# Filter spectra of the 256-step stream from even and odd lags, and expert weights in groups of four rows

## The chip, the cores and the metric

The kernel runs on one core of a Trainium2 chip. The metric is the device time of one execution in microseconds (us); the time of a kernel is the median of its runs. TensorE (PE in the profile, its weight loads are PEld), VectorE (DVE), ScalarE (ACT), GpSimd (POOL) and SyncE (SP) run their own instruction streams and meet at semaphores. The DMA engines move data between HBM and SBUF.

## What is computed

A two-layer step over two streams, a context of 128 tokens and a latent grid of 256 tokens, both 1024 wide, all in float32. Layer 0 mixes tokens with long convolutions (Hyena), layer 1 with a gated scan (RG-LRU); after each comes a mixture of 16 experts, of which a token takes two. The parts of the reference that matter here:

```python
def hyena_filter_spectrum(length, f_w1, f_b1, f_freq, f_w2, f_b2, f_w3):
    ...
    h = (h @ f_w3.astype(f32)).reshape(length, 2, HY_ORDER, D_MODEL)
    deltas = jnp.abs(jnp.linspace(MIN_DECAY, MAX_DECAY, D_MODEL, dtype=f32))
    h = h * jnp.exp(-t[:, :, None, None] * deltas)
    h_fwd = h[:, 0]
    h_bwd = h[1:, 1]
    norm = jnp.sum(jnp.abs(h_fwd), axis=0) + jnp.sum(jnp.abs(h_bwd), axis=0) + FILTER_EPS
    k = jnp.concatenate([h_fwd, jnp.zeros((1, HY_ORDER, D_MODEL), f32), h_bwd[::-1]], axis=0) / norm
    return jnp.fft.rfft(k, axis=0)

def moe_ffn(h, router_w, router_bias, w1, w3, w2):
    ...
    def expert_block(args):
        xblk, e = args
        return (jax.nn.silu(xblk @ w1[e]) * (xblk @ w3[e])) @ w2[e]
```

The kernel computes the transforms as matrix products with cosine and sine matrices (constants named `lag`, `fwd`, `inv`).

## The kernel before

**Tiles.** Tokens lie in three tiles of 128: tile 0 is the context, tiles 1 and 2 the latent stream. `halves` is the large SBUF buffer that holds weights, filters and spectra; `PS` is PSUM, eight banks of 512 floats per partition. A float32 `mm` is two matmul instructions in the trace, so 10 calls read as x20.

**Layer 0, the filters.** The filters are made in four units (convolution 0 or 1, channels 0-511 or 512-1023). For unit i, `filter_rows` (PE, six products, one per tile and direction) is windowed by DVE into `fa` and `fb` (sums and differences of the two directions). ACT takes absolute values (`filter_abs`, L559 and L560), DVE their larger (`filter_larger`, L1344), PE adds them up (`filter_sums`, 12 small products), DVE inverts (`filter_norm`). `spectrum(i)` on PE multiplies `fa` and `fb` by the lag matrices: for each of three frequency tiles ft and r = 0 (real, from `fa`), 1 (imaginary, from `fb`) one result ("K", i, ft, r) of 128x512. For ft = 0 (context) it is one product, for ft = 1 and 2 (latent) two products that accumulate, over lags 0-127 and 128-255. ACT copies all six results to `spec[i]` (`emptied`, L477).

**What sets the order.** Each engine runs a hand-written list (`mixer0` has one for PE, one for ACT, one for DVE). The results of the filter and transform work share banks 3 to 7: `pool_plan` numbers the uses in PE's order, use u gets bank 3 + u % 5, and PE's `take` for use u waits until use u - 5 has been emptied by the engine that the plan names. So the sixth result of a spectrum waits for the copy of its first, and the sums after it for the copy of its second. Between the units PE runs `in_tile(ct)` (24 input projection tiles), `ada` (modulation rows) and, from ct = 5, `z_rows`, `transform` and `inverse`; DVE multiplies the spectra in `multiply`. Unit 0's spectrum stands before `norm_spread(0)`, unit 1's after `mod_columns(0)`, unit 2's and 3's after `in_tile(1)` and `in_tile(3)`. On ACT the copies of unit 1 stand behind `modulate(0)` (L514) and those of units 2 and 3 behind `in_tile` and `filter_abs`.

**The experts.** SP loads per expert six pieces of 2 MB: the two halves of w1 and w3 alternating, then w2, each as [128 partitions x 4096 floats], into eight ring slots, each as soon as the slot's last reader is done. The view `(k p j) n -> p k (j n)` with j = 2 gives every partition two pairs of neighbouring rows, that is two stretches of 8 KB. PE for expert e multiplies by w1 and w3 (64 matmul instructions, L752 `halves,hT`), gathers the next expert's tokens out of `h` (12, `h,hT`), transposes hid (4) and gate picks (3), multiplies by w2 (32), transposes the gathered tokens `xg` (4, L756) and combines (16, `hT,misc`). `xg` columns must come in the order in which the weights' rows lie, so `chunk` picks every second column of a 256-column stretch. An expert with over 64 tokens has an extra pass. ACT writes `h` from transposed tokens in `token_tile` (L717), six per layer, the first of them ahead of the router's exponential.

```python
order = (("moe_w1", 0), ("moe_w3", 0), ("moe_w1", 1), ("moe_w3", 1), ("moe_w2", 0), ("moe_w2", 1))
MOE_RELEASE = ("w13_last", "w13_last", "w13_last", "w13_last", "w2_first", "w2_mm")
```

Of the kernel before, what the change touches and what calls it, by code (L numbers as in the profile page):

```python
# [11 lines left out]
ALU = mybir.AluOpType  # L12
ACT = mybir.ActivationFunctionType
AX = mybir.AxisListType.X

P = 128
# [48 lines left out]

def constants():
# [16 lines left out]
    for name, n in (("lat", LAT), ("ctx", CTX)):  # L83

        k = np.arange(n) if n == CTX else np.concatenate([np.arange(0, n, 2), np.arange(1, n, 2)])
# [8 lines left out]
        at = np.pi * (2 * k[None, :] + 1) * np.arange(n)[:, None] / (2 * n)  # L94
        lag.insert(0, np.stack([np.cos(at), -sign * np.sin(at)], 1).reshape(n // P, P, 2 * n).transpose(1, 0, 2)
                   .reshape(P, 2 * n * n // P))
# [4 lines left out]
    for n in (CTX, LAT):  # L101
        t = np.linspace(0.0, 1.0, n, dtype=np.float32)[:, None]
        w = np.float32(2.0 * math.pi / n) * np.arange(n, dtype=np.float32)[:, None]
        a = (bands * w).astype(np.float32)
        feats.append(np.concatenate([t, np.cos(a), -np.sin(a)], -1))
        window.append(np.exp(-t * deltas))
# [89 lines left out]
def pool_plan():  # L196
# [4 lines left out]
    spectrum = lambda i: [("act", ("K", i, ft, r)) for ft in range(NT) for r in range(2)]  # L201
# [21 lines left out]
def program(nc, A, y_prompt, y_sample, new_state):  # L223
    where, (pool, pool_order, pool_count) = plan(), pool_plan()
    with ExitStack() as ctx:
# [66 lines left out]
        lags = halves[:, W_AT + 6656:W_AT + 7936]  # L292
# [62 lines left out]
        def _(sp):  # L355
# [50 lines left out]
            for l in range(LAYERS):  # L406
# [10 lines left out]
                w = {m: A[m].rearrange("l e (k p j) n -> p (l e) k (j n)", p=P, j=2) for m in ("moe_w1", "moe_w3", "moe_w2")}  # L417
                order = (("moe_w1", 0), ("moe_w3", 0), ("moe_w1", 1), ("moe_w3", 1), ("moe_w2", 0), ("moe_w2", 1))

                def expert(c, e):  # L420
                    name, half = order[c]
                    return w[name][:, l * NE:(l + 1) * NE][:, bass.ds(e, 1), 2 * half:2 * half + 2, :]

                def load_expert(c, r, e, *released):
                    slot = moe_slot(r, c)
                    load(("moe", l, slot), expert(c, e), ring[:, slot, :].rearrange("p (o k n) -> p o k n", o=1, k=2),
# [34 lines left out]
        def _(act):  # L461
# [88 lines left out]
            def spectrum(i):  # L550
                for ft in range(NT):
# [151 lines left out]
            for l in range(LAYERS):  # L703
# [11 lines left out]
                def token_tile(i):  # L715
                    act.wait_ge(S("tok_mm"), before("tok_mm", l) + i + 1)
                    a.activation(h[:, i // 2, i % 2 * HALF:i % 2 * HALF + HALF], PS[:, 2 + i, :], ACT.Copy) \  # L717
                        .then_inc(S("tok"), 1)
# [31 lines left out]
        def _(pe):  # L750
# [53 lines left out]
            def spectrum(i):  # L804
                lat = lags[:, 2 * CTX:].rearrange("p (k r f) -> p k r f", k=2, r=2)
                pe.wait_ge(S("pl_dve"), pool["rows", i, NT - 1, 1][2])
                for ft in range(NT):
                    for r, src in enumerate((fa, fb)):
                        bank = take(("K", i, ft, r))
                        if ft == 0:  # L810
                            last = mm(PS[:, bank, :], lags[:, CTX * r:CTX * r + CTX], src[:, 0, :], True, True)
                        else:
                            for k in range(2):
# [1032 lines left out]
```

## Time and profile before

| | |
|---|---|
| median of 3 runs | 1675.11 us (1672.68 to 1677.9) |
| the profiled execution | 1676.27 us |
| its span in the trace | 1674.5 us |
| PE busy / DVE busy / ACT busy | 1555.0 / 713.3 / 331.6 us |
| moved by DMA | 495.66 MB in 83949 packets |

The span is the time from the first to the last instruction; 1.8 us lie outside. Layer 0's mixer ends at about 351 us, its experts fill 380 to 948 us, layer 1's mixer 950 to 1135 us, its experts 1165 to 1656 us. A row of the timeline is a start, a length, engine, line, operation and tiles, merged over neighbours of one kind; in brackets stands the idle time ahead and what ended it.

### The profile page before, as it was taken

How to read it: one execution, taken by the hardware profiler on the slowest of the kernel's cores; microseconds unless marked ns; L12 is line 12 of the kernel's file. 1: busy time of each engine (PE TensorE's matmuls, PEld its weight loads, DVE VectorE, ACT ScalarE, POOL GpSimd, SP SyncE). 2: the span in 40 equal slices, each digit the busy share in tenths (PEclk: the TensorE clock that was granted, in tenths of full speed). 3: DMA queues.
4: the chain of work that ended last, by engine and by line, in shares of the span. 5: the costliest groups of instructions: out<-in, count | busy, mean ns of one | idle time of the engine just before them, and what ended most of it. 6: DMA issues, size and time to landing. Idle time of an engine off the chain costs nothing.

```text
span 1674.5 us, 21517 instructions
## 1 busy us (share of the span) xinstructions
PE 1555.0 (93%) x7910; PEld 699.9 (42%) x7911; DVE 713.3 (43%) x2050; ACT 331.6 (20%) x539; POOL 0.2 (0%) x4
## 2 busy tenths in 40 slices
PE   6999999978999999999989799896999998999996
PEld 3454555543343333333333355453333333333333
DVE  3325665352424434334343548725334342434343
ACT  4322222030101111010101357413011110111111
POOL 0000000000000000000000000000000000000000
PEclk9999999989999999999999899997999999999998
DMA  9438776830858999999968501424799995999993
GB/s 351 153 106 299 264 262 226 349 153 1 354 249 336 423 422 422 422 422 422 422 267 350 201 0 51 201 101 163 288 413 422 422 422 240 423 422 421 423 423 132
DMA packets 83949, 495.66 MB, mean 296 GB/s; under 512 B 4465, under 2 KB 21121, under 8 KB 28225
## 3 DMA queue, kind: packets, MB, share of 16 engines
q1 hardware_dynamic: 82432, 489.33, 72.3%
q10 hardware_dynamic: 1472, 5.72, 1.0%
q8 instruction: 31, 0.51, 0.1%
q14 instruction: 14, 0.11, 0.0%
HBM read 493.45 MB, written 1.58 MB: 296 GB/s over the span
## 4 chain that ended last, share of the span: by engine, by line
PE 83%; DVE 6%; DMA 5%; ACT 3%; issue 2%; SPq 0%; DVEq 0%; ACTq 0%
PE PS L752 81%; DMA halves<-in_moe_w 4%; PE PS L756 2%; DMA halves<-in_ada_w 1%; DVE misc L1760 1%; ACT hT L543 1%; DVE xc L1702 1%; DVE misc L1522 0%; DVE halves L1522 0%; DVE halves L1513 0%; DVE halves L1515 0%; DVE halves L1514 0%; DVE hT L1750 0%; ACT hT L528 0%; ACT hT L514 0%
## 5 line engine op out<-in xcount | busy, mean ns | idle before, releaser
L752 PE MATMUL PS<-halves,hT 128*64 128x512 f32 x3072 | 677.0, 596 | 22.4 <-ACT hT L543 17.2
L752 PEld LDWEIGHTS PS<-halves,hT 128*64 128x64 f32 x3072 | 225.4, 137 | 442.5 <-issue 432.8
L752 PE MATMUL PS<-hT,halves 128*128 128x384 f32 x640 | 218.7, 497 | 8.4 <-ACT halves L626 6.5
L1702 DVE SCALAR_TENSOR_TENSOR xc<-PS,MOD,xc 128x128 f32<-128x128 f32 x592 | 195.8, 409 | 37.4 <-PE PS L752 37.4
L752 PEld LDWEIGHTS PS<-hT,halves 128*128 128x128 f32 x640 | 121.5, 193 | 106.7 <-issue 23.0
L1750 DVE TENSOR_TENSOR hT<-hT,PS 128x512 f32<-128x512 f32 x32 | 22.0, 688 | 279.3 <-ACT hT L528 279.3
L752 PE MATMUL PS<-halves 128*128 128x384 f32 (+1 forms) x336 | 118.5, 512 | 0.7 <-ACT pre L573 0.7
L752 PE MATMUL PS<-h,hT 128*64 128x512 f32 x408 | 108.8, 667 | 7.4 <-issue 3.9
L1760 DVE COPY misc<-PS 128x512 f32<-128x512 f32 x32 | 22.1, 692 | 216.6 <-PE PS L752 216.6
L528 ACT ACTIVATE hT<-PS 128x512 f32<-128x512 f32 x32 | 19.1, 597 | 449.6 <-PE PS L752 449.6
L752 PE MATMUL PS<-hT,misc 64*128 64x384 f32 x512 | 91.2, 495 | 3.6
L752 PEld LDWEIGHTS PS<-halves 128*128 128x128 f32 x336 | 63.4, 190 | 53.9 <-issue 17.1
L756 PEld LDWEIGHTS PS<-cst,hT 128*128 128x128 f32 x408 | 50.9, 185 | 58.9 <-issue 55.1
L548 ACT ACTIVATE hT<-PS 128x512 f32<-128x512 f32 x32 | 19.1, 597 | 244.8 <-PE PS L756 244.8
L756 PE MATMUL PS<-cst,hT 128*128 128x128 f32 x408 | 65.6, 296 | 1.7 <-DVE hT L1736 1.7
L752 PEld LDWEIGHTS PS<-h,hT 128*64 128x64 f32 x408 | 32.4, 153 | 75.6 <-issue 75.6
L752 PEld LDWEIGHTS PS<-hT,misc 64*128 64x128 f32 x512 | 46.8, 186 | 34.4 <-DVE misc L1760 9.7
L543 ACT ACTIVATE hT<-PS 128x512 f32<-128x512 f32 x32 | 19.1, 597 | 151.7 <-PE PS L756 151.7
L1318 DVE SCALAR_TENSOR_TENSOR h<-pre,VT,h 128x127 f32<-128x127 f32 (+1 forms) x80 | 29.7, 412 | 45.0 <-ACT h L577 28.6
L528 ACT ACT_TABLE_LOAD x32 | 41.1, 1283 | 33.2 <-issue 33.2
L752 PE MATMUL PS<-halves,cT 128*32 128x512 f32 x384 | 46.2, 598 | 0.6 <-DMA halves<-in_ada_w 0.6
L573 ACT ACTIVATE pre<-PS,VT 128x384 f32<-128x384 f32 x24 | 14.0, 581 | 165.3 <-PE PS L752 165.3
(232 smaller groups left out, 1107.5 us busy)
## 6 DMA issues: line engine op xcount, KB each, us to landing
halves<-in_moe_w SPq DMA_DIRECT2D x192, 2048.0 KB, 16.4
halves<-in_ada_w SPq DMA_DIRECT2D x48, 1024.0 KB, 6.9
halves<-in_hy_w_in SPq DMA_DIRECT2D x12, 1024.0 KB, 5.2
halves<-in_rg_w_in SPq DMA_DIRECT2D x4, 2048.0 KB, 15.5
halves<-in_hy_w_out SPq DMA_DIRECT2D x4, 1024.0 KB, 8.2
halves<-in_rg_w_out SPq DMA_DIRECT2D x2, 2048.0 KB, 9.7
halves<-in_rg_wa SPq DMA_DIRECT2D x1, 2048.0 KB, 11.4
halves<-in_rg_wx SPq DMA_DIRECT2D x1, 2048.0 KB, 15.2
```

What stands on the lines that cost most here:

```text
L528: a.activation(hid, PS[:, 2, :], ACT.Sigmoid).then_inc(S("sig"), 1)
L543: a.activation(hidT, PS[:, 5, :].rearrange("p (c m) -> p c m", m=P), ACT.Copy) \
L548: a.activation(xT, PS[:, 1, :].rearrange("p (c m) -> p c m", m=P), ACT.Copy).then_inc(S("xT"), 1)
L573: a.activation(pre[:, ct % 2, :], PS[:, ct % 2, 0:N], ACT.Identity, bias=VT[:, 0, HB + ct:HB + ct + 1]).then_inc(S("in_ev0"), 1)
L752: return nc.tensor.matmul(out, lhsT, rhs, start=start, stop=stop)
L756: return nc.tensor.transpose(out, in_, ident[0:n, 0:n])
L1318: last = v.scalar_tensor_tensor(o, i, weight, o, ALU.mult, ALU.add)
L1702: ins = v.scalar_tensor_tensor(xc[:, k, cs], PS[:, bank, cs], MOD[:, l, 8 * G2 + k, s:s + 1], xc[:, k, cs], ALU.mult, ALU.add)
L1750: ch.link(v.tensor_tensor(hid, hid, PS[:, 2, :], ALU.mult))
L1760: v.tensor_copy(yo, PS[:, 6, :]).then_inc(S("yo"), 1)
```

## The change

**Spectra.** Frequencies come in an even and an odd half, and the second half is now listed backwards (`np.arange(n - 1, 0, -2)`), so that frequency f of the first half stands beside its mirror image. `filter_times` lists the latent lags even first, then odd; features and window follow it. The even lags' sum E and the odd lags' sum O are each one product of 128 lags with 128 frequencies; the first half of the spectrum is E + O, the second E - O. PE thus makes six products per unit in place of ten, in the order K(0) twice, then for each r the odd sum (named ft = 2) and the even sum (ft = 1). ACT copies K(0) and the odd sums (four of six); the new DVE function `halves_joined` adds the even sum in PSUM to the copied odd sum and subtracts them. The lag matrices shrink from 1280 to 768 columns.

**Experts.** The view of w1 and w3 gets j = 4: every partition gets four neighbouring rows, one stretch of 16 KB per piece. w2 stays. `token_tile` writes the columns of `h` in the matching order, reading PSUM in steps of four floats, and the transposes of `xg` (and `Xxg` in extra passes) take plain stretches of 128 columns.

```diff
+def filter_times(n):
+    return np.arange(n) if n == CTX else np.concatenate([np.arange(0, n, 2), np.arange(1, n, 2)])
...
-        k = np.arange(n) if n == CTX else np.concatenate([np.arange(0, n, 2), np.arange(1, n, 2)])
+        k = np.arange(n) if n == CTX else np.concatenate([np.arange(0, n, 2), np.arange(n - 1, 0, -2)])
...
-        at = np.pi * (2 * k[None, :] + 1) * np.arange(n)[:, None] / (2 * n)
+        k, sign = k[0:P], sign[0:P]
+        at = np.pi * (2 * k[None, :] + 1) * filter_times(n)[:, None] / (2 * n)
...
-    spectrum = lambda i: [("act", ("K", i, ft, r)) for ft in range(NT) for r in range(2)]
+    spectrum = lambda i: [("act", ("K", i, 0, r)) for r in range(2)] + \
+        [(e, ("K", i, ft, r)) for r in range(2) for e, ft in (("act", 2), ("dve", 1))]
...
-                w = {m: A[m].rearrange("l e (k p j) n -> p (l e) k (j n)", p=P, j=2) for m in ("moe_w1", "moe_w3", "moe_w2")}
+                w = {m: A[m].rearrange("l e (k p j) n -> p (l e) k (j n)", p=P, j=j)
+                     for m, j in (("moe_w1", 4), ("moe_w3", 4), ("moe_w2", 2))}
...
-                    a.activation(h[:, i // 2, i % 2 * HALF:i % 2 * HALF + HALF], PS[:, 2 + i, :], ACT.Copy) \
-                        .then_inc(S("tok"), 1)
+                    a.activation(h[:, i // 2, i % 2 * HALF:i % 2 * HALF + HALF].rearrange("p (k c) -> p k c", k=4),
+                                 PS[:, 2 + i, :].rearrange("p (c k) -> p k c", k=4), ACT.Copy).then_inc(S("tok"), 1)
...
             def spectrum(i):
                 lat = lags[:, 2 * CTX:].rearrange("p (k r f) -> p k r f", k=2, r=2)
                 pe.wait_ge(S("pl_dve"), pool["rows", i, NT - 1, 1][2])
-                for ft in range(NT):
-                    for r, src in enumerate((fa, fb)):
-                        bank = take(("K", i, ft, r))
-                        if ft == 0:
-                            last = mm(PS[:, bank, :], lags[:, CTX * r:CTX * r + CTX], src[:, 0, :], True, True)
-                        else:
-                            for k in range(2):
-                                last = mm(PS[:, bank, :], lat[:, k, r, P * (ft - 1):P * ft], src[:, 1 + k, :],
-                                          k == 0, k == 1)
-                        last.then_inc(S("pl_mm"), 1)
+                for r, src in enumerate((fa, fb)):
+                    bank = take(("K", i, 0, r))
+                    mm(PS[:, bank, :], lags[:, CTX * r:CTX * r + CTX], src[:, 0, :], True, True).then_inc(S("pl_mm"), 1)
+                for r, src in enumerate((fa, fb)):
+                    for k in (1, 0):
+                        bank = take(("K", i, 1 + k, r))
+                        mm(PS[:, bank, :], lat[:, k, r, :], src[:, 1 + k, :], True, True).then_inc(S("pl_mm"), 1)
...
-                        last = tr(PS[:, 1, P * c:P * c + P], chunk(xg, c))
+                        last = tr(PS[:, 1, P * c:P * c + P], xg[:, P * c:P * c + P])
...
+            def halves_joined(i):
+                for r in range(2):
+                    odd = spec[i][r][:, 2, :]
+                    even = PS[:, source(("K", i, 1, r)), :]
+                    dve.wait_ge(S("pl_act"), pool["K", i, 2, r][2])
+                    link(v.tensor_tensor(spec[i][r][:, 1, :], even, odd, ALU.add))
+                    v.tensor_tensor(odd, even, odd, ALU.subtract).then_inc(S("pl_dve"), 1)
...
                 filter_larger(0)
+                halves_joined(0)
                 norm_apply(0)
```

`halves_joined(i)` follows `filter_larger(i)` on DVE for each of the four units; for unit 3 it stands ahead of `fold(0)`.

On PE, the stretch from the modulation rows to the first input tiles with the spectra of units 1 and 2. Before:

```order
12 L752 MATMUL PS<-halves,cT 32x512 x12
13 L756 MATMUL PS<-cst,RG 128x128 x4
14 L752 MATMUL PS<-halves 128x512 x10
15 L752 MATMUL PS<-cst,halves 128x32 x12
16 L752 MATMUL PS<-hT,halves 128x384 x8
17 L752 MATMUL PS<-halves,stack 128x512 x6
18 L752 MATMUL PS<-hT,halves 128x384 x8
19 L752 MATMUL PS<-halves 128x512 x10
20 L752 MATMUL PS<-cst,halves 128x32 x12
```

The same stretch after the change; here the file's lines are 12 higher:

```order
12 L764 MATMUL PS<-halves,cT 32x512 x12
13 L768 MATMUL PS<-cst,RG 128x128 x4
14 L764 MATMUL PS<-halves 128x512 x6
15 L764 MATMUL PS<-cst,halves 128x32 x12
16 L764 MATMUL PS<-hT,halves 128x384 x8
17 L764 MATMUL PS<-halves,stack 128x512 x6
18 L764 MATMUL PS<-hT,halves 128x384 x8
19 L764 MATMUL PS<-halves 128x512 x6
20 L764 MATMUL PS<-cst,halves 128x32 x12
```

Only the spectra change, from ten calls to six; nothing else moves on PE.

On DVE, unit 0 (`filter_larger` 128x1536, `norm_apply` x8). Before:

```order
21 L1284 RECIPROCAL rs<-rs 128x96
22 L1344 TENSOR_TENSOR halves<-halves 128x1536
23 L1291 TENSOR_TENSOR hT<-xc,PS 128x384 x8
24 L1348 TENSOR_SCALAR small<-PS 128x8
25 L1350 RECIPROCAL small<-small 128x8
```

After:

```order
21 L1294 RECIPROCAL rs<-rs 128x96
22 L1363 TENSOR_TENSOR halves<-halves 128x1536
23 L1357 TENSOR_TENSOR halves<-PS,halves 128x512
24 L1358 TENSOR_TENSOR halves<-PS,halves 128x512
25 L1357 TENSOR_TENSOR halves<-PS,halves 128x512
26 L1358 TENSOR_TENSOR halves<-PS,halves 128x512
27 L1301 TENSOR_TENSOR hT<-xc,PS 128x384 x8
```

The four new instructions stand between `filter_larger` and `norm_apply`.

## Rows read from the trace of the kernel before

**Rows 1.** The page's chain that ended last: shares of the span by line.
```profile
PE PS L752 81%; DMA halves<-in_moe_w 4%; PE PS L756 2%; DMA halves<-in_ada_w 1%; DVE misc L1760 1%; ACT hT L543 1%; DVE xc L1702 1%; DVE misc L1522 0%; DVE halves L1522 0%; DVE halves L1513 0%; DVE halves L1515 0%; DVE halves L1514 0%; DVE hT L1750 0%; ACT hT L528 0%; ACT hT L514 0%
```

**Rows 2.** Busy by stretch: span, PE, PEld, DVE, ACT, POOL, granted clock, DMA, GB/s.
```profile
160.00:200.00 40.00, 40.00 (x204) 22.15 (x203) 23.84 (x52) 9.22 (x16) 0.00 (x0) 1.00 0.70 256
```

**Rows 3.** Timeline of PE (and one PEld row) at the spectra of units 0 to 2.
```profile
26.93 8.85 PE L752 MATMUL PS<-halves 128*128 128x512 f32 x20
...
52.17 9.03 PE L752 MATMUL PS<-halves 128*128 128x512 f32 x20
...
59.22 0.30 PEld L752 LDWEIGHTS PS<-halves 128*128 128x128 f32 x2 [0.84 <-ACT halves L477]
...
61.04 2.76 PE L752 MATMUL PS<-cst,halves 128*128 128x32 f32 x24
...
79.19 8.75 PE L752 MATMUL PS<-halves 128*128 128x512 f32 x20
87.78 2.76 PE L752 MATMUL PS<-cst,halves 128*128 128x32 f32 x24
```

**Rows 4.** Timeline of ACT at the copies of units 0 to 2.
```profile
29.16 1.07 ACT L477 ACTIVATE halves<-PS 128x512 f32<-128x512 f32 x2
...
54.21 4.48 ACT L514 ACTIVATE hT<-hT,MOD,MODA 128x128 f32<-128x128 f32 x10
58.59 2.50 ACT L477 ACTIVATE halves<-PS 128x512 f32<-128x512 f32 x5
...
83.36 2.04 ACT L477 ACTIVATE halves<-PS 128x512 f32<-128x512 f32 x4
```

**Rows 5.** Timeline of DVE: norm_apply beside unit 0, filter_larger of unit 2.
```profile
36.68 3.81 DVE L1291 TENSOR_TENSOR hT<-xc,PS 128x384 f32<-128x384 f32 x8 [5.63 <-PE PS L752]
...
83.49 1.76 DVE L1344 TENSOR_TENSOR halves<-halves,h 128x1536 f32<-128x1536 f32 x1 [1.22 <-ACT h L560]
```

**Rows 6.** Timeline of PE, products with w1 and w3: unbroken, and the last broken one.
```profile
725.03 13.95 PE L752 MATMUL PS<-halves,hT 128*64 128x512 f32 x64
...
813.16 7.09 PE L752 MATMUL PS<-halves,hT 128*64 128x512 f32 x32
821.12 7.09 PE L752 MATMUL PS<-halves,hT 128*64 128x512 f32 x32 [0.87 <-DMA halves<-in_moe_w]
```

**Rows 7.** Busy by stretch (columns of rows 2), where the weight stream starts again.
```profile
508.00:510.00 2.00, 2.00 (x8) 0.65 (x6) 0.66 (x3) 0.00 (x0) 0.00 (x0) 0.50 0.50 74
```

**Rows 8.** DMA packets: 560 to 740 us (experts), 948 to 956 us (in_rg_wx).
```profile
DMA packets 9860, 75.97 MB, mean 422 GB/s; under 512 B 587, under 2 KB 587, under 8 KB 587
...
DMA packets 2729, 2.79 MB, mean 349 GB/s; under 512 B 16, under 2 KB 2728, under 8 KB 2728
```

**Rows 9.** Timeline, all engines, after an expert's w2; last row: token-tile transposes.
```profile
1253.51 0.74 PE L756 MATMUL PS<-cst,hT 128*128 128x128 f32 x4
1253.62 0.69 DVE L1760 COPY misc<-PS 128x512 f32<-128x512 f32 x1 [6.76 <-PE PS L752]
...
1254.36 2.24 PEld L752 LDWEIGHTS PS<-hT,misc 64*128 64x128 f32 x16 [0.31 <-DVE misc L1760]
...
1146.73 0.66 PE L756 MATMUL PS<-cst,hT 128*128 128x128 f32 x4
```

**Rows 10.** Timeline, all engines, layer 1's router.
```profile
1147.42 0.60 ACT L717 ACTIVATE h<-PS 128x512 f32<-128x512 f32 x1
...
1149.48 2.53 ACT L717 ACTIVATE h<-PS 128x512 f32<-128x512 f32 x5
...
1159.38 4.88 PE L752 MATMUL PS<-h,hT 128*64 128x512 f32 x12 [1.72 <-DVE hT L1694]
```

**Rows 11.** Busy by stretch (columns of rows 2) around PE's longest single wait.
```profile
1074.00:1078.00 4.00, 0.08 (x1) 0.00 (x0) 3.90 (x8) 0.00 (x0) 0.00 (x0) 1.00 1.01 422
1078.00:1080.00 2.00, 0.00 (x0) 0.00 (x0) 1.46 (x4) 0.50 (x2) 0.00 (x0) 0.57 1.02 426
1080.00:1084.00 4.00, 3.46 (x6) 1.95 (x7) 2.80 (x5) 2.53 (x6) 0.00 (x0) 0.50 0.07 23
```

More of the change, by code:

```diff
@@ L93, in constants @@
         put("inv_" + name, inv.reshape(2 * n // P, P, half).transpose(1, 0, 2))
-        at = np.pi * (2 * k[None, :] + 1) * np.arange(n)[:, None] / (2 * n)
-        lag.insert(0, np.stack([np.cos(at), -sign * np.sin(at)], 1).reshape(n // P, P, 2 * n).transpose(1, 0, 2)
-                   .reshape(P, 2 * n * n // P))
+        k, sign = k[0:P], sign[0:P]
+        at = np.pi * (2 * k[None, :] + 1) * filter_times(n)[:, None] / (2 * n)
+        lag.insert(0, np.stack([np.cos(at), -sign * np.sin(at)], 1).reshape(n // P, P, 2 * P).transpose(1, 0, 2)
+                   .reshape(P, 2 * n))
     feats, window = [], []
@@ L104, in constants @@
         a = (bands * w).astype(np.float32)
-        feats.append(np.concatenate([t, np.cos(a), -np.sin(a)], -1))
-        window.append(np.exp(-t * deltas))
+        feats.append(np.concatenate([t, np.cos(a), -np.sin(a)], -1)[filter_times(n)])
+        window.append(np.exp(-t * deltas)[filter_times(n)])
     feats = np.ascontiguousarray(np.concatenate(feats, 0).T, np.float32)
@@ L291, in program @@
         fa, fb, fab = tok3(W_AT + 2048), tok3(W_AT + 3584), tok3(W_AT + 5120)
-        lags = halves[:, W_AT + 6656:W_AT + 7936]
+        lags = halves[:, W_AT + 6656:W_AT + 6656 + 2 * N]
         zf = [halves[:, W_AT + 2048 * hh:W_AT + 2048 * hh + 4 * N].rearrange("p (b n) -> p b n", b=4) for hh in range(2)]
@@ L421, in expert @@
                     name, half = order[c]
-                    return w[name][:, l * NE:(l + 1) * NE][:, bass.ds(e, 1), 2 * half:2 * half + 2, :]
+                    n = w[name].shape[2] // 2
+                    return w[name][:, l * NE:(l + 1) * NE][:, bass.ds(e, 1), n * half:n * half + n, :]
                 def load_expert(c, r, e, *released):
                     slot = moe_slot(r, c)
-                    load(("moe", l, slot), expert(c, e), ring[:, slot, :].rearrange("p (o k n) -> p o k n", o=1, k=2),
+                    load(("moe", l, slot), expert(c, e), ring[:, slot, :].rearrange("p (o k n) -> p o k n", o=1, k=1 if c < 4 else 2),
                          *released)
@@ L550, in spectrum @@
             def spectrum(i):
-                for ft in range(NT):
+                for ft in (0, 2):
                     for r in range(2):
@@ L1099, in extra_pass @@
                     for c in range(2):
-                        last = tr(PS[:, 1, P * c:P * c + P], chunk(Xxg, c))
+                        last = tr(PS[:, 1, P * c:P * c + P], Xxg[:, P * c:P * c + P])
                     last.then_inc(S("x_xT_mm"), 1)
@@ L1186, in expert_layer @@
                         for c in range(4):
-                            last = tr(PS[:, 1, P * c:P * c + P], chunk(xg, c))
+                            last = tr(PS[:, 1, P * c:P * c + P], xg[:, P * c:P * c + P])
                         last.then_inc(S("xT_mm"), 1)
@@ L1331, in filter_rows @@
                 if i:
-                    dve.wait_ge(S("pl_mm"), pool["K", i - 1, NT - 1, 1][0] + 1)
+                    dve.wait_ge(S("pl_mm"), pool["K", i - 1, 1, 1][0] + 1)
                 else:
@@ L1371, in multiply @@
                     x, y = terms[:, ft % 2 * 2, :], terms[:, ft % 2 * 2 + 1, :]
-                    dve.wait_ge(S("pl_act"), pool["K", i, ft, 1][2])
+                    dve.wait_ge(S("pl_dve" if ft else "pl_act"), pool["K", i, min(ft, 1), 1][2])
                     v.tensor_tensor(x, Kr[:, ft, :], p, ALU.mult)
@@ L1417, in mixer0 @@
                 filter_larger(1)
+                halves_joined(1)
                 filter_norm(1)
@@ L1422, in mixer0 @@
                 filter_larger(2)
+                halves_joined(2)
                 short_conv0(2)
@@ L1427, in mixer0 @@
                 filter_larger(3)
+                halves_joined(3)
                 fold(0)
```

1 line of the change is left out of this document (removed).

## Prediction

> **What bounds the kernel now.** Read the page's chain first [rows 1]: 83% of the span is PE in the lines of `mm` and `tr`, 4% waits for expert weights, and DVE and ACT appear with single per cents. Then the stretches: in the filter stage PE is busy 40.00 of 40 us at clock 1.00 while DVE has 16 us free [rows 2]. So in layer 0's mixer a PE instruction that goes is worth its full length, unless PE then meets a wait that it was too slow to meet before. Third, the timeline of PE at the spectra, beside those of ACT and DVE [rows 3 to 5], for those waits. Fourth, the experts: two unbroken groups of 32 take 13.95 us, but the last three experts before layer 0's fourth extra pass break in the middle and wait for DMA [rows 6].
>
> **Spectra on PE.** Twenty instructions take 8.75 to 8.85 us when nothing stops them, so one call (two instructions) is 0.86 us. Four calls per unit go: 3.4 us, 13.7 us over four units. How much of it is kept is read unit by unit, in times of before counted from the spectrum's start. The copies on ACT run at 0.50 to 0.54 us each, the first ending 0.60 us after its start [rows 4].
>
> Unit 0 [rows 3]: start 26.93. The sixth call now wants its bank at 26.93 + 5 x 0.86 = 31.2; ACT's first copy starts at 29.16 and ends near 29.8 [rows 4]. No wait. The full 3.4 us is kept, if nothing behind it is late. DVE now runs four 128x512 instructions ahead of `norm_apply`. They cost 0.69 us each, by the PSUM copy of the same shape [rows 9]. The last needs the sixth call (32.1) and a copy, and ends near 34.1; `norm_apply` starts at 36.68 today [rows 5], so it still moves 2.6 us forward, and PE needs its result only at the first input tile, 25 us on. Cover: if DVE were 3 us slower here, that tile's 25 us would still hide it.
>
> Unit 1: start 52.17. ACT must finish `modulate(0)` first; its copies start at 58.59 whatever PE does, the first ends at 59.19, and PE waited 0.84 us (by the weight loader) for it at 59.22 already before [rows 3, 4]. Now PE has five calls done at 56.5 and stands 2.7 us. Only the sixth result is shorter, one call in place of two: the sums move from 61.04 to 60.18, 0.86 us kept.
>
> Unit 2: start 79.19. ACT copies from 83.36, first done 83.96; the sixth call wants 83.5 and gets 84.0, done at 84.9. The sums then need `filter_larger`, 83.49 + 1.76 = 85.25 [rows 4, 5]. So they start at 85.3 in place of 87.78: 2.45 us kept. Unit 3 repeats this 28.8 us later: 2.45. What is late next in both is ACT's `filter_abs`, not the new DVE work: `halves_joined` stands behind `filter_larger`, ends about 3 us after it, and its banks are wanted by `filter_rows` only after a further input tile of 5 us.
>
> Sum: 3.4 + 0.86 + 2.45 + 2.45 = 9.2 us. The 16 new DVE instructions (11 us) and the eight copies that ACT loses count nothing, under the 16 us in 40 of free DVE time. The lag load shrinks by 0.26 MB in a start that moves some 420 GB/s: 0 to 0.6 us, taken as 0, since `ada(0)` arrives on the other queue. Bounds of this part: 13.7 if ACT's copies turn out no limit, 6 if each unit loses a further 0.8 us to late banks.
>
> **Expert weights.** The DMA rate depends on the row length [rows 8]: 16 engines need 16 x 180 / 9860 packets, 0.292 us each, for mostly 8 KB rows, and 16 x 8 / 2729 = 0.0469 us for mostly 1 KB rows. A line through both (bytes 75.97 and 2.79 MB) gives 9.4 ns per packet and 36.7 ns per KB (1000 bytes). An expert is 12.58 MB in 6 x (256 + 16) = 1632 packets: (461.7 + 15.3) / 16 = 29.81 us, while PE needs 28.73 us for an expert. With 16 KB rows the four pieces of w1 and w3 have 144 packets: 1120 in all, (461.7 + 10.5) / 16 = 29.51 us, 0.30 less. This extrapolates beyond 8 KB; it is an estimate from rows. The stream started again at 509 [rows 7] and PE's last wait ended at 821.12: 10.8 expert times, so the weights come 3.2 us earlier there. The three breaks cost 0.86, 1.04 and, shown, 821.12 + 7.09 - 813.16 - 13.95 = 1.10 us: 3.0 us, just covered, so all three go: 3.0 kept. Layer 1 has no such wait: nothing. Below: 0 if 16 KB rows run as 8 KB ones; above 3.0 there is nothing to gain.
>
> The Trainium skill, page "DMA: Bandwidth & Descriptors", section "Why small descriptors are slow (HBM only)", has a fixed overhead of about 3 cycles per packet; with its fabric clock of 850 MHz that is 3.5 ns where the rows say 9.4. By it an expert would gain 0.11 us, the last wait would move by 1.2 us, about half the wait time would stay, and the result would be 1.5 to 2 us higher than mine. That is a rival below.
>
> **The order of `h`.** Transposes of `xg` in steps of two take 0.74 us for four, those of the token tiles in plain columns 0.66 [rows 9]. The four plain ones save 0.08 us in each of 32 experts, but the combine does not start when they end: it starts at 1254.36, released by the copy of yo that ends at 1254.31, and this copy does not change [rows 9]. Kept: only where transposes stand on the path alone, twice at a layer's start and in five extra passes, 0.3 us. If all counted it would be 2.9. The Trainium skill, page "SBUF — State Buffer", section "Door 1: The DMA port swizzle", says that a step costs nothing while two accesses hit the same 16 bytes, so a step of two floats would be free and this term 0; the 0.74 against 0.66 speaks against that.
>
> `token_tile` reads PSUM in steps of four floats; no row shows ACT doing that. The first tile, at 1147.42 [rows 10], stands just ahead of the router's exponential, on the path; the other five end at 1152.0, 7 us before the gather that needs them. Bounds: 0, or twice the time, 0.6 us on the first tile per layer, 1.2 in all; I take 0, nearest to ACT's plain read of the same size.
>
> **Sum.** 9.2 + 3.0 + 0.3 = 12.5 us. The profiled execution has a span of 1674.5 and lasted 1676.27; it becomes 1662.0 and 1663.8. It lay 1.2 us over the median, so against 1675.11 the forecast is 1662.6 us.
>
> **Rivals.**
> A, the DMA term is missing or halved: 16 KB rows cost what 8 KB rows cost, or the per-packet cost is smaller. For: no row is longer than 8 KB in a clean stretch. Against: the line between 1 and 8 KB. Time 1664.4 to 1665.6. Chance 0.16.
> B, PE's new wait in unit 1 pulls the clock. PE's longest single wait kept clock 1.00 for its first 4 us and fell to 0.50 after that, for some 5 us [rows 11]. The new wait is 2.7 us between two busy stretches, so I expect 1.00; if it falls, 4 us at half rate cost 2 us, and a late bank more: 1664.6 to 1667. Chance 0.09.
> C, more is kept: transposes count in every expert, or ACT's copies let PE through: 1659 to 1660.5. Chance 0.07.
> D, slower than before: one 16 KB stretch per partition makes HBM or the engines slower than two of 8 KB. Place: layer 0's 10.8 experts before 821 us lose x us each, and layer 1's two unbroken stretches (some 7 and 8 experts, each near its limit: 8 x 1.08 = 8.6 us behind at the end, without a wait) lose about 7x - 1.4 and 8x - 0.3. The 9.5 us of the other terms are gone when 26x = 11.2, at x = 0.43: 30.2 us per expert, 416 GB/s in place of 422. At 30.5 us (412 GB/s) the kernel takes 1682. For: nothing in a row; against: the same line. Chance 0.04.
> E, the change does not shorten the filters: the new order makes every unit wait for ACT as unit 1 does, 0.9 us each, in place of 9.2. Then 1668 to 1671. Against: only unit 1 has `modulate` ahead of its copies. Chance 0.04.
>
> **How the numbers follow.** The forecast, within 1.5 us of 1662.6, has 0.60. Range 1658.8 to 1667.5: the lower end takes in C, the upper A and most of B, with the runs' own spread of 2.4 us. A measurement tells 0.3%, 5 us, from no change. Faster by more than that (under 1670.1) are the forecast, A, B, C and most of E: 0.93. Same: the rest of E and a mild D: 0.04. Slower: 0.03.
>
> **What would show it.** Filter stage: the sums of unit 0 start 3.4 us earlier, of unit 1 4.3, unit 2 6.7, unit 3 9.2 us, and the end of the mixer (351 us) too; a PE wait of 2.7 us for ACT in unit 1, clock 1.00; DVE waits for no one new. Experts: about 425 to 427 GB/s, 67600 packets in all, no wait for in_moe_w1 or w3 before the fourth extra pass, 28.73 us per expert as before. Transposes of xg 0.66 us, combine still released by DVE's copy. ACT's token tiles 0.60 us. The forecast is wrong if PE waits for DVE's sums and differences, if experts take other than 28.73 us without waits, or if the DMA rate stays at 422.

## The result and the profile after

The changed kernel is slower: 1692.33 us median of four runs (1683.19 to 1698.53) against 1676.51 for the kernel before on the same chip, ratio 1.0091 with a 95% interval of 1.0069 to 1.0113. The forecast was 1662.6. The profiled execution is the fastest of the four, 1683.19 us with a span of 1681.4. It has one stall; by their times the three others, from 1691.9 us on, have two, as the runs below suggest.

The filter stage, timeline of PE (start, duration, engine, line, operation, count, idle time before and its releaser), answers to [rows 3]:

```profile
26.98 5.42 PE L764 MATMUL PS<-halves 128*128 128x512 f32 x12
...
48.79 4.46 PE L764 MATMUL PS<-halves 128*128 128x512 f32 x10
55.84 1.13 PE L764 MATMUL PS<-halves 128*128 128x512 f32 x2 [2.59 <-ACT halves L488]
56.80 4.19 PE L764 MATMUL PS<-cst,halves 128*128 128x32 f32 x24
60.80 7.33 PE L764 MATMUL PS<-hT,halves 128*128 128x384 f32 x16
67.97 5.31 PE L764 MATMUL PS<-halves,stack 128*128 128x512 f32 x12
...
83.08 1.12 PE L764 MATMUL PS<-halves 128*128 128x512 f32 x2 [0.35 <-ACT halves L488]
84.39 2.87 PE L764 MATMUL PS<-cst,halves 128*128 128x32 f32 x24 [0.19 <-DVE halves L1363]
...
110.81 3.83 PE L764 MATMUL PS<-cst,halves 128*128 128x32 f32 x24 [0.19 <-DVE halves L1363]
114.57 3.64 PE L764 MATMUL PS<-halves,cT 128*32 128x512 f32 x16
```

Starts behave as forecast: unit 1's spectrum begins 3.38 us earlier, its sums 56.80 in place of 61.04. But the 24 sums take 4.19 us where they took 2.76, and the input tile behind them 7.33 where units without trouble show 5.41. At 67.97 only 0.9 us of the 4.2 is left (before, that row starts at 68.88). Unit 3 repeats it (3.83, and 3.64 for a row that takes 1.92 before). The stretches say why; columns are those of [rows 2], the clock is the third figure from the right:

```profile
53.00:57.00 4.00, 1.41 (x6) 0.68 (x5) 0.15 (x1) 4.00 (x10) 0.00 (x0) 1.00 1.07 408
58.00:61.00 3.00, 3.00 (x15) 3.00 (x16) 1.55 (x3) 0.00 (x0) 0.00 (x0) 0.50 1.03 421
61.00:64.00 3.00, 3.00 (x5) 1.63 (x6) 0.37 (x2) 0.00 (x0) 0.00 (x0) 0.50 0.22 90
64.00:68.00 4.00, 4.00 (x13) 2.27 (x12) 0.00 (x0) 0.00 (x0) 0.00 (x0) 0.91 0.00 0
...
114.00:118.00 4.00, 4.00 (x20) 1.10 (x19) 1.27 (x3) 0.00 (x0) 0.00 (x0) 0.50 0.21 31
```

During the wait the granted clock is 1.00; PE then works again, and from 58 to 64 us the clock is 0.50, the lower of its two levels. The mixer ends 2.6 us early (its follow-up, 64 entries of h,cst, starts at 348.87, before at 351.50), not 9.2.

The experts: the DMA of 560 to 740 us (answers to [rows 8]), and then the timeline of PE (to [rows 6]).

```profile
DMA packets 6796, 76.71 MB, mean 426 GB/s; under 512 B 578, under 2 KB 578, under 8 KB 578
```

```profile
775.63 13.95 PE L764 MATMUL PS<-halves,hT 128*64 128x512 f32 x64
...
804.37 13.95 PE L764 MATMUL PS<-halves,hT 128*64 128x512 f32 x64
...
941.00 0.54 PE L764 MATMUL PS<-h,cst 128*32 128x96 f32 x16
```

The groups of w1 and w3 are whole and 28.74 us apart, with no wait for weights, and layer 0's experts end 6.84 us early (before at 947.84). Then layer 1, PE's timeline around 1338 us:

```profile
1334.64 0.66 PE L768 MATMUL PS<-cst,hT 128*128 128x128 f32 x4
1335.50 2.85 PE L764 MATMUL PS<-hT,misc 64*128 64x384 f32 x16 [0.20 <-DVE misc L1783]
1349.54 16.61 PE L764 MATMUL PS<-halves,hT 128*64 128x512 f32 x64 [11.18 <-issue]
```

PE stands 11.2 us at a turn of the loop, from its second expert back to its first, and waits for nothing that the profile shows ("issue"). The DMA rows (packets, MB, share of the engines) show two packets of 16 KB of instructions in that moment, from 1338 to 1340 us (first row), and ten from 1230 us to the end (second); in the kernel before the latter stretch has none. The third row is the page's, where the kernel before has 31:

```profile
q8 instruction: 2, 0.03, 11.8%
...
q8 instruction: 10, 0.16, 0.2%
...
q8 instruction: 40, 0.66, 0.2%
```

Nine of the ten come between 1339 and 1409 us, about one trip through the loop, and one at its end, at 1662 us. So the loop's code, which the kernel before reads once, in its first trip, was read again in the middle of the loop. DVE and ACT wait for PE meanwhile.

### The profile page after: what moved, and what is told of

Its sections match the earlier page's. It is cut to its first block, busy times and chain, and to the rows that moved or that the text cites. A ratio compares the mean times of both kernels' runs of the same rounds, so it can differ in the third digit from the quotient of the medians.

```text
span 1681.4 us, 21469 instructions
## 1 busy us (share of the span) xinstructions
PE 1546.0 (92%) x7878; PEld 691.5 (41%) x7879; DVE 723.3 (43%) x2066; ACT 326.8 (19%) x531; POOL 0.2 (0%) x4
## 2 busy tenths in 40 slices
DMA packets 67573, 495.55 MB, mean 295 GB/s; under 512 B 4464, under 2 KB 21120, under 8 KB 28224
## 4 chain that ended last, share of the span: by engine, by line
PE 85%; DVE 7%; ACT 4%; issue 2%; DMA 1%; DVEq 0%; SPq 0%; ACTq 0%
PE PS L764 82%; PE PS L768 3%; DMA halves<-in_ada_w 1%; DVE misc L1783 1%; DVE xc L1725 1%; ACT hT L554 1%; ACT hT L525 0%; ACT halves L570 0%; DVE halves L1545 0%; DVE misc L1545 0%; DVE halves L1538 0%; DVE halves L1536 0%; DVE halves L1363 0%; DVE halves L1537 0%; DVE hT L1773 0%
## 5 line engine op out<-in xcount | busy, mean ns | idle before, releaser
L764 PE MATMUL PS<-halves 128*128 128x384 f32 (+1 forms) x304 | 105.3, 505 | 4.0 <-ACT halves L488 3.3
L764 PEld LDWEIGHTS PS<-halves 128*128 128x128 f32 x304 | 57.2, 190 | 50.2 <-issue 8.7
L768 PEld LDWEIGHTS PS<-cst,hT 128*128 128x128 f32 x408 | 46.6, 163 | 61.0 <-issue 57.3
## 6 DMA issues: line engine op xcount, KB each, us to landing
halves<-in_rg_wa SPq DMA_DIRECT2D x1, 2048.0 KB, 11.2
halves<-in_rg_wx SPq DMA_DIRECT2D x1, 2048.0 KB, 13.7
```

The source lines that it names most:

```text
L764: return nc.tensor.matmul(out, lhsT, rhs, start=start, stop=stop)
L768: return nc.tensor.transpose(out, in_, ident[0:n, 0:n])
```

## The experiments

Two losses are to be explained: the stall with its second fetch, and the clock. Theory 1 on the stall: the spectra's 16 removed calls shorten PE's instruction stream ahead of the expert loops, and how the loop's code (some 1640 places, counting four for each call, which the trace shows as two multiplications and two weight loads, and one for each other instruction) lies in blocks of 256 decides whether it stays in PE's instruction memory. (A place is the room of one instruction; the 1640 are my count from the kernel, no trace gives them.) Theory 2: the 16 KB weight rows do it. The Trainium skill, page "Runtime: NRT & Kernel Launch", section "Instruction fetch mechanics", has the memory refilled in blocks of 16 KiB, 256 instructions, with 2048 instructions for PE. It says that a taken branch to a target outside the current window of two pages waits for a fetch. The trace agrees with the block: 31 packets are 0.51 MB. It does not agree with the two pages: in the kernel before, the loop of some 6.4 blocks turns back time after time behind 1222 us, and no packet comes.

### Parts apart

**The filter part alone.** The experts' part is taken back:

```diff
-                w = {m: A[m].rearrange("l e (k p j) n -> p (l e) k (j n)", p=P, j=j)
-                     for m, j in (("moe_w1", 4), ("moe_w3", 4), ("moe_w2", 2))}
+                w = {m: A[m].rearrange("l e (k p j) n -> p (l e) k (j n)", p=P, j=2) for m in ("moe_w1", "moe_w3", "moe_w2")}
...
-                        last = tr(PS[:, 1, P * c:P * c + P], xg[:, P * c:P * c + P])
+                        last = tr(PS[:, 1, P * c:P * c + P], chunk(xg, c))
...
```

> Only the filter part of the change: the spectra from even and odd lags; the experts' weights, the transposes of xg and the token tiles are as before. PE's instruction stream in front of both expert loops is then shorter by 16 calls, as in the changed kernel. Theory 1 (the 11.2 us stall of layer 1 is a second fetch of PE's loop code, and it comes from where this code lies in the stream): the stall is here too, and the median is 7 to 25 us above what the parts give (1672), so 1680 to 1695, in the range of the changed kernel. Theory 2 (the 16 KB rows of the weights disturb the fetch): no stall; the filter stage keeps only 2.6 us as in the changed kernel's profile, so 1672 to 1674. In both the clock falls to 0.5 to 0.6 for some us after PE's wait in unit 1.

Ten runs fall in two groups: 1667.1, 1670.1, 1670.6, 1671.0, 1671.7 and 1678.8, 1684.3, 1684.6, 1685.4, 1686.1; median 1675.24, ratio 1.0005 (0.9974 to 1.0035). Four or five runs carry something of some 14 us, the size of one stall. If that is what it is, the 16 KB rows aren't needed for it, but it is rarer than in the changed kernel. The only trace kept is of the lower group and has no stall in the loops, so this rests on the times. Its clock is 0.50 from 56.5 to 66.7 us.

**The experts' part alone.** The kernel before with the other half of the diff.

> Only the experts' part: first and third matrices in fours, plain columns for the transposes of xg, stepped reads in the token tiles; the filters are as before and so is the place of every PE instruction. Theory 1 (place of the code): no second fetch of instructions, all three breaks for weights in layer 0 gone, 1671 to 1673. Theory 2 (16 KB rows): the 11 us stall appears here as well, 1682 to 1692.

Median 1675.08, ratio 0.9994 (0.9982 to 1.0006); ten runs from 1672.4 to 1680.9, none in an upper group. In the trace the three breaks are gone, the stream carries 426 GB/s from 560 to 740 us, and PE's last row is

```profile
1656.52 4.18 PE L758 MATMUL PS<-cst,xc 128*128 128x128 f32 x24 [3.45 <-DVE xc L1704]
```

These transposes start 3.1 us before those of the kernel before (1659.64): the size forecast. But this is the fastest of the ten runs. Over all runs the gain is 1 us with 2 of uncertainty, so the times don't show the 3.3 us forecast; the section on the prediction separates it from the clock. At the old place of the code, 16 KB rows alone cause no stall: theory 2 falls as the sole cause.

### The place of the loop code

**The changed kernel, padded by 64 places.**

```diff
             mm(PS[0:64, 1, 0:N], f_w1, features, True, True).then_inc(S("f_mm"), 1)
+            for _ in range(64):
+                pe.wait_ge(S("f_in"), 16)
...
                 mm(PS[:, 1, 0:N], f_w2, f_h1, True, True).then_inc(S("f_mm"), 1)
+                for _ in range(64):
+                    pe.wait_ge(S("f_in"), 16)
```

Two such waits make one instruction, so these are 64 instructions.

> The changed kernel with 64 waits that are already met put into PE's stream in two of its idle times before the first spectrum (32 each), so that every instruction behind the filters stands as many entries from the start as in the kernel before. Theory 1 (place of the code): the second fetch goes, and what is left is the changed kernel without stall: 1669 to 1671.5 (1662.6 forecast, and 6.4 us lost to the clock in units 1 and 3). Theory 2 or chance: as the changed kernel, 1683 to 1699.

1669.33 us (six runs, 1664.2 to 1671.7), ratio 0.9949 (0.993 to 0.9968): as theory 1 said. 32 instructions in each of two idle times of PE at the start take 23 us off the changed kernel (the medians are of two rounds; by the ratios to the kernel before it is 24). Its trace has 31 packets of instructions, and PE's timeline no gap at the same turn of the loop:

```profile
1333.88 2.85 PE L764 MATMUL PS<-hT,misc 64*128 64x384 f32 x16 [0.20 <-DVE misc L1787]
1336.66 13.53 PE L764 MATMUL PS<-halves,hT 128*64 128x512 f32 x62
```

**The kernel before, padded by 192 places**, 64 behind the first product and 128 behind the second, in the same way (384 waits in pairs), so that its loops stand in their blocks as in the changed kernel:

> The kernel before with 192 waits that are already met in PE's two idle times before the first spectrum (64 and 128), so that the expert loops' code stands, counted in blocks of 256 instructions (16 KB, the size of one fetch in the trace), where it stands in the changed kernel. Theory 1: the kernel before now shows the second fetch of loop code and PE stalls of about 11 us, 1684 to 1700. Theory 2 or another cause: 1675 to 1680, the waits costing 0 to 4 us of their own.

Nine runs: six from 1681.0 to 1687.5, and 1702.6, 1711.2, 1718.1; median 1685.99, ratio 1.006 (1.0028 to 1.0093). The added waits cost more than expected, some 90 ns for each instruction of two: the 128 behind the second product fill 12.3 us, where PE stood 5.1 before, and PE's first work behind them starts at 25.5 in place of 16.9 us. That is the lower group. The other three lie 19, 28 and 35 us above that group's 1683; the kernel before itself had 69 runs beside the kernels of this section, and none above 1680.5. So by the times the place alone brings losses like the stalls, without the change, in a third of the runs. No trace of such a run was kept, and the three don't lie in steps of 13 us.

**The changed kernel again**, unaltered, on another chip:

> The changed kernel once more, unaltered, on a second chip beside the kernel before. If its stalls come from the place of PE's loop code, single runs lie in steps of some 12 to 15 us above the 1669 of the padded one: most between 1683 and 1699. If the four runs seen were chance, it is near 1669 to 1676.

1695.22 (1694.2 to 1699.9), ratio 1.011 (1.0083 to 1.0138). Here PE's timeline in the profiled run has two stalls, and the page 49 packets of instructions:

```profile
1233.26 16.96 PE L764 MATMUL PS<-halves,hT 128*64 128x512 f32 x64 [11.09 <-issue]
...
1618.87 15.31 PE L764 MATMUL PS<-halves,hT 128*64 128x512 f32 x64 [10.75 <-issue]
```

Against 1669.3 this is 26 us for two, 13 each: 11 of standing, the rest in short waits of the code's next trip and a lower clock behind the gap. Each stall brings nine packets. It comes at a turn of layer 1's loop, but not always at the same one (1338 us in the first profile; 1222 and 1608 here).

**The changed kernel moved by one whole block**, by 64 tiny multiplications of four places each:

```diff
+            for _ in range(26):
+                mm(PS[0:64, 0, 0:4], f_w1, features[:, 0:4], True, True)
...
+                for _ in range(38):
+                    mm(PS[0:64, 0, 0:4], f_w1, features[:, 0:4], True, True)
```

> The changed kernel with 64 tiny multiplications (64x4 outputs, into a bank that is free then) in PE's two idle times before the first spectrum. As one call fills four places of the instruction stream, all code behind them moves by 256 instructions, one whole block. Theory 1 (the place within a block decides): the stalls stay, 1683 to 1700 in most runs. Rival (any added instructions, or the idle time they fill, cure it): 1668 to 1672, as with 64 added places.

1701.37 (1697.8 to 1704.0), ratio 1.0139 (1.0112 to 1.0166), again two stalls of 11.15 and 10.84 us in the profile. More instructions at the start don't cure it; what counts is the place within a block.

**Moved by 32 and by 128 places** in the same way, with 8 and with 32 multiplications:

> The changed kernel with 8 tiny multiplications, 32 places, half of the 64 that cured it. No theory says where the edge lies: with the edge between 32 and 64 it stalls as the changed kernel (1690 to 1700), with the edge below 32 it is as the padded one, 1668 to 1671.

> The changed kernel with 32 tiny multiplications, 128 places, half a block: twice the 64 that cured it. If only a narrow stretch of places is bad, 1668 to 1672; if the good stretch is the narrow one, 1690 to 1703.

1669.33 (four runs, 1664.8 to 1670.0, ratio 0.9947) and 1669.9 (ten runs, 1667.1 to 1675.2, ratio 0.9966): both free of it. Shifts of 32, 64 and 128 places are good, 0 and 256 bad: an edge lies within 32 places of where the change put the loops, another between 128 and 256.

The packets show the place themselves. In all seven profiles of kernels at the bad place, with and without stalls and whichever half of the change they hold, one packet comes 0.5 to 1.1 us before the last products of layer 1's loop end: at 1662.0 us in the changed kernel, at 1651.1 with the filter part alone, at 1662.7 in the kernel before with its padding. In the eight other profiles no packet comes after layer 1's first trip. So at the bad place PE asks for a further block just ahead of the loop's end. That a stall is this request made at a turn, before the branch back is taken, is my reading; no run separates it.

### What the rows of 16 KB add

**The experts' part alone at the bad place**, by 20 and 28 of the tiny multiplications, and then **the kernel before** with the same:

> Only the experts' part of the change, with 48 tiny multiplications (64x4 outputs, 192 places) in PE's two idle times before the first spectrum, so that the loop code stands within its block of 256 instructions where it stands in the changed kernel. Theory 1 with the rows of 16 KB raising the number of second fetches: nearly every run has one or two stalls of 11 us, 1688 to 1705. Theory 1 alone: stalls in a third to a half of the runs, as the rows of 8 KB showed, median 1676 to 1688. Without stall it is 1675 to 1678.

> The kernel before with the same 48 tiny multiplications (192 places) as the run with the experts' part alone, so the two differ in the experts' part (rows of 16 KB in place of 8 KB for the first and third matrices, and the order of h) and nothing else. If the rows of 16 KB make the second fetch more frequent: stalls in a third to a half of the runs, one mostly, median 1676 to 1690. If the rows do nothing: two stalls in every run, 1697 to 1703, and the milder results of the filter part alone and of the padding with waits had another cause.

The experts' part alone at the bad place: 1699.39, all four runs from 1697.6 to 1701.0, ratio 1.0136 (1.0118 to 1.0154), two stalls in the profile. The kernel before at that place: 1676.46, ratio 1.0022 (0.9999 to 1.0045); ten of twelve runs lie between 1671.2 and 1679.7, two at 1692.0 and 1694.1. The two kernels differ in the experts' part alone. In their profiles the instructions from 1230 us on are 19 packets with the experts' part, nine for each stall and the one at the loop's end, and that one alone without:

```profile
q8 instruction: 19, 0.31, 0.3%
```

```profile
q8 instruction: 1, 0.02, 0.0%
```

The place thus makes a second fetch possible, and the experts' part makes it near certain, and mostly double. By their times all 16 runs at the bad place with rows of 16 KB have it, and with rows of 8 KB 9 or 10 of 31 have a loss like it (4 or 5 of 10, 3 of 9, 2 of 12). All seven stalls that a trace shows are with rows of 16 KB. Alone, each half of the change ends at the time of the kernel before; the filter part loses its gain in half of its runs. Whether it is the 16 KB packets, between which a fetch must find its turn, or the stream's other timing wasn't separated.

### The clock

**Unit 1 kept busy.** In the padded kernel, with 12 paddings fewer (the loop of 64 waits behind the first product becomes 40), the fifth call is made four times over:

```diff
                     for k in (1, 0):
                         bank = take(("K", i, 1 + k, r))
+                        for _ in range(3 if i in (1,) and (r, k) == (1, 1) else 0):
+                            mm(PS[:, bank, :], lat[:, k, r, :], src[:, 1 + k, :], True, True)
```

> The padded changed kernel, and in unit 1 the spectrum's fifth call is made four times over (three more calls of 0.86 us, 12 places; 12 paddings fewer), so PE multiplies through the 2.6 us in which it waited for ACT. Theory (that wait pulls the clock): granted clock 1.00 in the ten microseconds behind, 24 sums in 2.8 us in place of 4.5, the tile behind them in 5.4 in place of 7.0, so all later work 3.3 us earlier: 1666 in place of 1669.3, though nothing that PE waits for comes earlier. Rival (the sums are slow because of the new VectorE or ScalarE work, or DMA beside them): the sums still take 4.2 to 4.5 us and the time stays 1669.

1664.73 (1662.9 to 1666.1), ratio 0.9919 (0.9897 to 0.9941): 4.6 us less than the padded kernel (on another chip; the two profiles' spans differ by 3.4), for 2.6 us more of PE work. PE's timeline, and the stretch behind the sums' start:

```profile
48.66 8.18 PE L764 MATMUL PS<-halves 128*128 128x512 f32 x18
56.68 2.76 PE L764 MATMUL PS<-cst,halves 128*128 128x32 f32 x24
59.27 5.41 PE L764 MATMUL PS<-hT,halves 128*128 128x384 f32 x16
```

```profile
58.00:61.00 3.00, 3.00 (x19) 2.34 (x19) 1.80 (x5) 0.00 (x0) 0.00 (x0) 1.00 0.98 410
```

The sums begin 0.6 us before those of the padded kernel (57.28), take 2.76 us again, and the clock stays at 1.00, with DVE and DMA about as busy beside them (1.80 and 0.98, before 1.55 and 1.03). The wait is what pulled the clock in unit 1. In unit 3 of this profile it still falls, from 110.6 us on for 3.4 us.

**The copies ahead of modulate(0).**

```diff
                 filter_abs(1)
-                modulate(0)
                 spectrum(1)
+                modulate(0)
```

> The padded changed kernel with one swap on ScalarE: the four copies of unit 1's spectra ahead of the ten instructions of modulate(0) (4.5 us). PE's wait of 2.6 us in unit 1 should go: copies from 51.4 us on, the sixth call at 53.5 with no wait, sums from 54.6 in place of 57.3, clock 1.00. modulate(0) then ends near 58, still ahead of the first input tile (59 or later). Kept: 2.6 us of wait and 3.3 us of clock, so 1669.3 - 5.9 = 1663.4. If modulate(0) becomes late, PE waits before the first input tile instead, up to 2 us.

1666.83 (1662.0 to 1674.1), ratio 0.9936 (0.9919 to 0.9953). The spectrum runs through and the sums start at 55.11, but `modulate(0)` now ends at 59.4, so PE waits 1.65 us before the first input tile, and the clock is 0.50 from 60.6 to 64.0 us. PE's timeline:

```profile
55.11 2.76 PE L764 MATMUL PS<-cst,halves 128*128 128x32 f32 x24
59.52 7.09 PE L764 MATMUL PS<-hT,halves 128*128 128x384 f32 x16 [1.65 <-issue]
```

I had put its end at 58; the copies wait for PE themselves (0.90 us on the fourth). In this profile, the slowest of the eight runs, unit 2's sums, behind waits of 0.35 and 0.19 us only, are slow too (3.91 us), which they weren't in the padded kernel (2.87).

**No wait in any unit.**

```diff
-            def spectrum(i):
-                for ft in (0, 2):
+            def spectrum(i, fts=(0, 2)):
+                for ft in fts:
...
                 filter_abs(1)
+                spectrum(1, (0,))
                 modulate(0)
-                spectrum(1)
+                spectrum(1, (2,))
                 for ct in range(24):
+                    if ct in (1, 3):
+                        filter_abs(2 + ct // 2)
                     in_tile(ct)
                     if ct in (1, 3):
-                        filter_abs(2 + ct // 2)
                         spectrum(2 + ct // 2)
```

> The padded changed kernel with three moves on ScalarE: in unit 1 two of the four spectrum copies stand ahead of modulate(0) and two behind it; in units 2 and 3 filter_abs stands ahead of the input tile's two instructions. Theory: PE's waits of 2.6 us in unit 1 and of 0.35 and 0.19 us in units 2 and 3 go, and modulate(0) still ends (57.5) before the sums do (57.9); with no wait the clock stays at 1.00 in all four units. Kept against the padded kernel's 1669.3: 2.6 + 3.3 (clock, unit 1) + 1.1 + some 2 (clock, units 2 and 3, in part of the runs) = 9.0, so 1660.3. If the clock falls for another reason than these waits, 1664 to 1666.

1662.79 us (five runs, 1658.5 to 1663.4), ratio 0.9905 (0.9888 to 0.9921): it beats the kernel before by 15.9 us by the ratio, 14.1 by the medians, and the changed kernel by some 30. PE's timeline in units 1, 2 and 3 and at the mixer's end:

```profile
49.61 5.32 PE L766 MATMUL PS<-halves 128*128 128x512 f32 x12
54.76 2.76 PE L766 MATMUL PS<-cst,halves 128*128 128x32 f32 x24
57.36 5.41 PE L766 MATMUL PS<-hT,halves 128*128 128x384 f32 x16
...
72.91 5.31 PE L766 MATMUL PS<-halves 128*128 128x512 f32 x12
78.06 2.76 PE L766 MATMUL PS<-cst,halves 128*128 128x32 f32 x24
...
103.41 2.76 PE L766 MATMUL PS<-cst,halves 128*128 128x32 f32 x24
...
338.12 1.83 PE L766 MATMUL PS<-h,cst 128*32 128x96 f32 x64
```

No row has a wait, the clock is 1.00 in every stretch to 131 us, and the mixer ends 13.4 us before that of the kernel before (351.50), nearly the 13.7 that the four removed calls of each unit take. The 1660.3 expected was 2.5 too low. That it comes out at the number forecast for the changed kernel is chance.

What is not shown is that the short waits of units 2 and 3 pull the clock. In unit 3 it fell in five of the nine profiles that have them and in none of the six without; three profiles show 0.50 for 3.4 us (from 36.7, 37.9 and 48.3 us on) with no wait of PE over 0.15 us in the 19 us before.

## Why the prediction was wrong

The sum was 12.5 us of gain; measured are 15.8 us of loss, from 1676.51 to 1692.33. The result lies 29.7 us above the forecast, and the runs divide that: 23.0 us are stalls (1692.33 against 1669.33 padded), and 6.7 lie between the padded kernel and the forecast, of which 4.6 (3.4 in the traces) are unit 1's clock.

**The step that failed first is one that wasn't there.** "Spectra on PE" priced the four removed calls per unit by their time on PE and nothing else ("Four calls per unit go: 3.4 us"). That they also move all code behind them by 64 places had no term. The chance of 0.03 for slower rested on rival D, slower rows of DMA, and D did not happen. A hint was to be had from the page before: its q8 queue fetches instructions in 16 KB packets, 31 in all, six of them between 1178 and 1222 us, in layer 1's first trip, and none from there to the end. With a loop of some 6.4 blocks that says that the code stays resident, and invites the question by what margin.

**Rival B was right in its mechanism and wrong in chance and price.** The step "PE's longest single wait kept clock 1.00 for its first 4 us ... so I expect 1.00" took [rows 11] for a free allowance: a wait of under 4 us would cost no clock. The wait came as sized (2.59, forecast 2.7) and the clock was 1.00 through it, but fell 2.0 us after it ended. What [rows 11] show is when the fall came there, not how short a wait escapes it. Priced at 2 us, unit 1 lost 3.3 in the trace and 4.6 over the runs. Units 2 and 3 had no such rival: behind their waits of 0.54 us together the clock fell in some executions (unit 3 in the changed kernel, 114 to 118 us in the rows; unit 2 in the reordered one) and not in others.

**Right, term by term.** Kept per unit before the clock: 3.38 (3.4), 0.86 (0.86), 2.48 (2.45) and 2.46 (2.45); the last two from the spectra's and the sums' starts, 78.28 and 84.39 against [rows 3], 104.69 and 110.81 against 107.98 and 116.56. `halves_joined` costs 0.68 to 0.69 us an instruction and PE waits for it nowhere; PE's new waits are for ACT's copy (0.35) and DVE's `filter_larger` (0.19), as named. The stream carries 426 GB/s with 67,573 packets (67,600), the three breaks are gone, an expert takes 28.73 us. The transposes of `xg` take 0.66 us, the combine is still released by DVE's copy, and ACT's first token tile takes 0.60 us with its steps of four.

**The experts' term, and the clock.** Between the ends of mixer and experts, layer 0's experts gained 4.2 us in the changed kernel (2.63 early before, 6.84 behind) and 2.4 with their part alone (0.50 and 2.94), but only 0.6 in the padded one (5.41 and 6.03). That stretch takes 588.8 to 597.0 us in the fifteen profiles, and the clock is at 0.50 for 27 to 44 us of it, in kernels of either kind, so one pair of profiles can't show 3 us. An estimate takes half of PE's busy time at 0.50 off each: the eleven profiles with rows of 16 KB then lie at 576.0 to 578.8 (mean 576.9) and have no wait for weights, the four with rows of 8 KB at 578.9 to 580.2 (mean 579.4) with two or three such waits, 1.5 to 2.4 us. That is 2.5 us for a term of 3.0. The same estimate for whole spans gives 1639.6 for the kernel before, 1627.6 to 1628.7 for the changed one moved by 32, 64 and 128 places, 10.9 to 12.0 us less (12.5 forecast); 1630.0 for the filter part alone (9.6 less, 9.2 forecast) and 1635.5 for the experts' part (4.1 less, 3.3 forecast). So most of what the changed kernel lacks of its forecast, the stalls apart, is the clock.

**The rate of DMA.** The line through [rows 8] held beyond 8 KB: 16 x 180 / 6796 packets is 0.424 us for a packet of 11.29 KB on average, and the line gives 0.424. So rival A, nothing or less from longer packets, did not happen.

So the model of the dependencies held to 0.1 us in the filters' starts, and the time was decided by two things outside it.

**Open.** Where exactly in the block the bad stretch ends, and which property of the experts' part makes the second fetch frequent. Also what picks the turn: of the seven stalls three come at 1338 to 1340 us, two at 1607 to 1608, one each at 1222 and 1551, all in layer 1; layer 0's loop has none.

## What to carry to other kernels

An edit in a long straight stretch moves the code of every loop behind it; count the instruction packets per stretch, before and after. If a run has more than one trip's worth, if a packet comes at the end of a loop that had none there, or if single runs lie in steps of a fixed size, move the loop by a few dozen places with cheap instructions in an idle time ahead before judging the edit. Make more than a few runs: one profile showed half of this loss. When PE gets faster in front of a wait, take the clock behind the new wait into the sum, or reorder the engine that it waits for, so that no wait arises; here dummy work in the gap already paid. And before a few us are read from one pair of profiles, compare the time at the lower clock in both.

## What was not expected of the hardware

- A second reading of a loop's code costs PE some 11 us at once (10.7 to 11.7 in seven stalls) and about 13 in the end. By their times, none of 73 runs of the kernel before has one and all eight of the changed kernel have; 32 places more ahead of the loop removed it.
- Two halves of a change that cost nothing alone (1.0005 and 0.9994) can cost 0.9 to 1.1% together, by way of a resource that neither names.
- Granted clock: in all seven profiles with the wait of 2.6 us it is 1.00 through the wait, falls to 0.50 between 0 and 2.7 us after its end, while PE is fully busy, and stays there for 6.8 us in five and 10.2 in two. In some executions it is 0.50 in 114 to 118 us, after waits of 0.35 and 0.19 us; that these cause it isn't shown.
- Waits that are already met aren't free on PE: about 90 ns for an instruction of two, 192 such instructions some 8 us beyond the idle time that they stood in.
